# A transformer kernel on one core: expert rows gathered from two tables instead of one

## The reference, cut to what matters

```python
q = (xb @ wq).reshape(t, PEER_HEADS, 2, PEER_DQ // 2)
s = jnp.einsum('thpd,hpkd->thpk', q, subkeys).astype(jnp.float32)
s_top, i_top = lax.top_k(s, K)
cand = (s_top[:, :, 0, :, None] + s_top[:, :, 1, None, :]).reshape(t, PEER_HEADS, K * K)
c_top, c_idx = lax.top_k(cand, K)
...
e = i1 * N_KEYS + i2
g = jax.nn.softmax(c_top, axis=-1)
ue = jnp.take(u, e, axis=0)
ve = jnp.take(v, e, axis=0)
act = jax.nn.gelu(jnp.einsum('thkd,td->thk', ue, xb).astype(jnp.float32), approximate=False)
return jnp.einsum('thk,thkd->td', (g * act).astype(xb.dtype), ve)
```

## Time and profile before

| | |
|---|---|
| median of two runs | 1958.32 us |
| the two runs | 1958.12 and 1958.52 us |
| span of the profiled execution | 1954.8 us |
| time around the span (median less span) | 3.5 us |
| busy: PE, DVE, ACT, POOL | 1688.8, 1292.9, 926.7, 826.3 us |
| bytes moved | 637.60 MB, mean 326 GB/s |
| issues of expert rows | 512 |
| granted TensorE clock | 0.987 of full, the level of 2.4 GHz, in all stages |

### The profile page before, as it was taken

How to read it: one execution, slowest core, us unless ns; L and a number is a source line. 1 busy time by engine, 2 the same in 40 slices (tenths; PEclk the granted TensorE clock), 3 DMA queues, 4 the chain that set the end, 5 groups by cost and what they waited for, 6 DMA issues and landing times.

```text
span 1954.8 us, 22618 instructions
## 1 busy us (share of the span) xinstructions
PE 1688.8 (86%) x7638; PEld 1040.0 (53%) x7638; DVE 1292.9 (66%) x2806; ACT 926.7 (47%) x2424; POOL 826.3 (42%) x756
## 2 busy tenths in 40 slices
PE   7998998877787788799899999989989778787777
PEld 7996444422332222399899999974444223232222
DVE  4568777666776665558745784488767666666644
ACT  5456554444544444466525344465454444444443
POOL 3335334433333333277615474653434333343331
PEclk9999999999999999999999999999999999999999
DMA  7548999999999999654303334789999999999996
GB/s 250 184 159 325 414 421 421 421 421 421 421 421 421 422 421 422 274 167 155 108 22 99 119 95 139 264 302 414 422 420 421 422 421 422 422 420 422 422 421 290
DMA packets 102052, 637.60 MB, mean 326 GB/s; under 512 B 11264, under 2 KB 12544, under 8 KB 36144
## 3 DMA queue, kind: packets, MB, share of 16 engines
q0 software_dynamic: 75216, 543.73, 67.1%
q1 hardware_dynamic: 26720, 92.43, 14.5%
HBM read 635.07 MB, written 1.05 MB: 325 GB/s over the span
## 4 chain that ended last, share of the span: by engine, by line
PE 42%; DMA 36%; DVE 12%; ACT 8%; issue 2%; POOL 0%; SPq 0%; ACTq 0%; DVEq 0%
DMA arena<-in_uv,arena 34%; PE pb L657 17%; PE pb L397 6%; PE pb L399 5%; PE pb L398 5%; DVE arena L1817 4%; ACT arena L1112 3%; PE pb L476 1%; PE pb L872 1%; DVE parts L1385 1%; DMA spare<-in_uv,arena 1%; PE pb L794 1%; PE pb L785 1%; ACT parts L958 1%; ACT arena L1107 1%
## 5 line engine op out<-in xcount | busy, mean ns | idle before, releaser
L657 PE MATMUL pb<-arena 128*128 128x512 f32 x1904 | 931.3, 620 | 209.7 <-ACT arena L1112 208.6
L1817 DVE SCALAR_TENSOR_TENSOR arena<-arena,pb 128x1024 f32<-128x1024 f32 x476 | 580.3, 1219 | 372.2 <-DMA arena<-in_uv,arena 372.0
L2325 POOL DMA_INDIRECT arena<-in_uv,arena x476 | 450.4, 946 | 726.4 <-PE pb L657 694.9
L657 PEld LDWEIGHTS pb<-arena 128*128 128x128 f32 x1904 | 332.5, 191 | 766.6 <-ACT arena L1112 510.0
L2299 POOL TENSOR_TENSOR parts<-ring,parts 128x512 fp32r<-128x512 f32 x222 | 327.9, 1500 | 312.5 <-ACT parts L958 311.5
L1104 ACT ACTIVATE arena<-arena 128x1 f32<-128x1 f32 x512 | 103.1, 201 | 579.5 <-DVE arena L1817 532.9
L958 ACT ACTIVATE parts<-ring 128x512 fp32r<-128x512 f32 x300 | 180.4, 627 | 174.0 <-PE pb L399 149.1
L397 PE MATMUL pb<-xl,parts 128*128 128x256 f32 x704 | 220.6, 313 | 11.3 <-POOL parts L2299 4.4
L1112 ACT ACTIVATE arena<-cst,arena 128x128 f32<-128x128 f32 x512 | 205.5, 401 | 48.3 <-ACT arena L1107 1.9
L399 PE MATMUL pb<-xh,parts 128*128 128x256 f32 x704 | 201.4, 286 | 0.0
L398 PE MATMUL pb<-xh,parts 128*128 128x256 f32 x704 | 201.3, 286 | 0.0
(11 more groups left out here) (329 smaller groups left out, 1677.5 us busy)
## 6 DMA issues: line engine op xcount, KB each, us to landing
ring<-in_w_in SPq DMA_DIRECT2D x108, 512.0 KB, 3.6
ring<-in_wq SPq DMA_DIRECT2D x18, 512.0 KB, 4.4
ring<-in_w_out SPq DMA_DIRECT2D x16, 512.0 KB, 3.8
arena<-in_uv,arena POOLq DMA_INDIRECT x476, 20.1
arena<-in_wq SPq DMA_DIRECT2D x10, 512.0 KB, 5.7
ring<-in_wa SPq DMA_DIRECT2D x8, 512.0 KB, 3.7
ring<-in_wb SPq DMA_DIRECT2D x8, 512.0 KB, 3.6
spare<-in_wq SPq DMA_DIRECT2D x4, 512.0 KB, 4.9
```

The lines of the kernel that those rows point to most:

```text
L657: ins = pe.matmul(ys[hf][:, :], diags[:, k % 4, :], lands[land_of[k]][:, D + hf * 512:D + (hf + 1) * 512], start=False, stop=k % (8 * K) = ...
L1817: ve.scalar_tensor_tensor(z, z, 1.0, xg[t], ALU.mult, ALU.mult, accum_out=hidden[:, k:k + 1]).then_inc(*up("v_dot", ("dot", e, k)))
L2325: gp.indirect_dma_start(lands[land_of[k]], None, rows_uv, bass.IndirectOffsetOnAxis(ap=eidx[:, k:k + 1], axis=0)).then_inc(*up(f"dma_rows{ ...
```

## The change

The table `uv` is given up for two tables, `u` and `v`, of 4 KB rows. Each slot takes two indirect DMAs with the same column of indices: first the `u` row into the first half of the place, with the semaphore and key `rows`, then the `v` row into the second half, with a new semaphore for each place and the key `values`. The dot product still waits for `rows`, which now stands for the first half alone. The matmuls wait for `values` as well as the diagonal. SP's wait before the second block's weights is now for the last `values`. The same bytes are moved.

```diff
--- before.py
+++ after.py
@@ -653,6 +653,7 @@
                         lend(("xg", e, 1), (0, 1))
                         ys = sums_begun(1)
                     pq.wait_ge(*on(("diag", e, k)))
+                    pq.wait_ge(*on(("values", e, k)))
                     for hf in range(2):
                         ins = pe.matmul(ys[hf][:, :], diags[:, k % 4, :], lands[land_of[k]][:, D + hf * 512:D + (hf + 1) * 512],
                                         start=False, stop=k % (8 * K) == 8 * K - 1)
@@ -2306,7 +2307,7 @@
             gp.dma_start(wab[:, :], d["wab"]).then_inc(*up("dma_wab", "ld_wab", 16))
             ahead(18 * 4 - PARTS + 4)
 
-            def experts(e, wq, out_features, sk, normed_rows, final_rows, rows_uv):
+            def experts(e, wq, out_features, sk, normed_rows, final_rows, rows_u, rows_v):
                 gq.wait_ge(*on(("full", (out_features, 3))))
                 gp.dma_start(keys.rearrange("p (b c) n -> p b (c n)", b=2), sk.rearrange("b p n -> p b n")).then_inc(
                     *up("dma_keys", ("keys", e), 16))
@@ -2322,11 +2323,14 @@
                         if land_used[k] is None and land_of[k] >= 7 and (plan[h][0], (n + 1) // 2) == (wq, land_of[k] - 6):
                             for p in pieces_of[h]:
                                 gq.wait_ge(*on(("lo", p)))
-                    gp.indirect_dma_start(lands[land_of[k]], None, rows_uv,
+                    gp.indirect_dma_start(lands[land_of[k]][:, 0:D], None, rows_u,
                                           bass.IndirectOffsetOnAxis(ap=eidx[:, k:k + 1], axis=0)).then_inc(
                         *up(f"dma_rows{land_of[k]}", ("rows", e, k), 16))
-
-            experts(1, "wq", "w_out", d["sk"], d["ffn1"], d["fin1"], d["uv"])
+                    gp.indirect_dma_start(lands[land_of[k]][:, D:2 * D], None, rows_v,
+                                          bass.IndirectOffsetOnAxis(ap=eidx[:, k:k + 1], axis=0)).then_inc(
+                        *up(f"dma_values{land_of[k]}", ("values", e, k), 16))
+
+            experts(1, "wq", "w_out", d["sk"], d["ffn1"], d["fin1"], d["u"], d["v"])
 
 
 
@@ -2355,7 +2359,7 @@
             for _ in range(len(fillers) - EARLY - 1):
                 item()
             ahead(8 * 4 - PARTS + 4)
-            experts(2, "wq2", "w_out2", d["sk2"], d["ffn2"], d["fin2"], d["uv2"])
+            experts(2, "wq2", "w_out2", d["sk2"], d["ffn2"], d["fin2"], d["u2"], d["v2"])
 
 
 
@@ -2386,7 +2390,7 @@
                     for p in pieces_of[before]:
                         sq.wait_ge(*on(("lo", p)))
                 if (name, i) == ("w_in2", 0):
-                    sq.wait_ge(*on(("rows", 1, NT * 8 * K - 1)))
+                    sq.wait_ge(*on(("values", 1, NT * 8 * K - 1)))
                 sp.dma_start(ring_of(k), d[name][i]).then_inc(*up(f"w_slot{ring_no[k] % SLOTS}", None, 16))
             for t in range(NT):
                 for hf in range(2):
...
```

More of the change, by code:

```diff
@@ L2443, in weight @@
         return np.ascontiguousarray(w.transpose(3, 0, 2, 1, 4)).reshape(2 * n, P, 1024)
-    def side_by_side(u, v):
-        return np.concatenate([u.reshape(P * P, D), v.reshape(P * P, D)], axis=1)
     def keys(s):
@@ L2472 @@
         "w_in": weight(a["w_in"][0], 14), "w_out": weight(np.roll(a["w_out"][0], 512, axis=0), 4), "wq": weight(a["peer_wq"][0], 8),
-        "sk": keys(a["peer_subkeys"][0].reshape(16, P, P)), "uv": side_by_side(a["peer_u"][0], a["peer_v"][0]),
+        "sk": keys(a["peer_subkeys"][0].reshape(16, P, P)), "u": a["peer_u"][0].reshape(P * P, D), "v": a["peer_v"][0].reshape(P * P, D),
         "ffn1": np.broadcast_to(a["norm_ffn_g"], (P, D)), "ffn2": np.broadcast_to(a["norm2_2"], (P, D)),
@@ L2476 @@
         "w_out2": weight(a["w_out_2"][0], 4), "wq2": weight(a["w_pq_2"][0], 8), "sk2": keys(sk2),
-        "uv2": side_by_side(a["expert_u_2"][0], a["expert_v_2"][0]),
+        "u2": a["expert_u_2"][0].reshape(P * P, D), "v2": a["expert_v_2"][0].reshape(P * P, D),
     }
```

## The result

| | before | after |
|---|---|---|
| median of the runs | 1958.32 us | 2174.70 us (2173.96 and 2175.45) |
| ratio, 95% interval | | 1.1095 (1.1077 to 1.1113) |
| span of the profiled execution | 1954.8 us | 2173.6 us |
| granted TensorE clock, mean | 0.987 | 0.905 |

The changed kernel is 216 us slower. I had forecast 45, and 2174.7 lies far outside my range of 1973 to 2032: the direction was right, the size was not. The 171 us that are missing are over four times the largest term of my sum (38.4).

The account below looks back on a forecast made before the run. The prediction took the 16 full DMA engines in the two expert stages as the bound, 2.492 us a slot. 38.4 + 9 - 2.6 = 45 us, with span 1954.8 and 3.5 around it, made 2003 us, range 1973 to 2032.

Parts of the forecast that it names:

- Packets: Expert stages' gathers: two 4 KB packets cost 1.03 times one of 8 KB, 0.075 us more a slot, 38.4 us.
- the 408 GB/s: Sign in the plateaus: DMA share stays at 1.00 and the rate falls from 421 to about 408 GB/s.
- GpSimd's issues: Each slot takes two indirect issues of 1.247 us, so GpSimd needs 2.49 us a slot instead of 1.25.
- Ten stops of GpSimd at fixed counts: GpSimd's five stops a stage, 2.3 us each, go by instruction count and become ten, 23 us a stage.
- my own sign of a forecast that is wrong altogether: GpSimd's stops don't double, or the issue of a half costs less than 0.94 us.
- The coupling: DMA and GpSimd paths without reserve lose a quarter of long slot waits: 4.4 us a stage, 9 in all, at most 17.5 a stage.
- Rival 3: GpSimd becomes the bound, stops and slot waits exposed: stage 686 instead of 653 us, +66 in all, 2024; chance 0.17.
- share below 0.97 with GpSimd busy without gaps: Sign that GpSimd has become the bound: DMA share drops below 0.97 while GpSimd is busy without gaps.
- The split's gain: At each stage's end the last dot product starts before the second half lands: 1.3 us gained a stage, 2.6 in all.
- rule of at least 1 MiB a DMA: Skill page's rule, about 2 us fixed for each DMA: 3.2 us for each half megabyte if run one after another.

Follow-up runs that it names:

- e8: Kernel before, with only the odd slots fetched as two gathers of 4 KB rows from separate tables, on one semaphore: 1980.5 us (ratio 1.0116).
- e5: Kernel before, with a second gather of 128 rows of 64 bytes behind the odd slots' gathers only: 1983.9 us (ratio 1.0133).
- e10: Changed kernel, with a 0.84 us subtraction on GpSimd in front of every second slot's gathers, a break after four gathers: 2137.9 us.
- e4: Kernel before, with a second gather of 128 rows of 64 bytes, read by nobody, behind every slot's gather: 2155.0 us.
- e12: Kernel before, with only each stage's last slot split into two gathers, its dot product behind the first half: 1955.6 against 1959.2 us.
- e1: Changed kernel, with both gathers of a slot on one semaphore, the dot product waiting for both and no extra TensorE wait: 2167.4 us.
- e3: Changed kernel with seven places instead of ten, so at most 14 gathers in flight instead of 20: 2171.7 us.
- e11: Changed kernel with five places instead of ten, so at most ten gathers in flight: 2172.9 us.
- e7: Kernel before, with a 0.84 us subtraction on GpSimd behind every slot's gather and no further DMA: 1970.9 us (ratio 1.0065).
- e6: Kernel before, with a second gather of 128 rows of 64 bytes in three slots of four: 2015.9 us (ratio 1.0297).
- e9: Changed kernel, with a 0.84 us subtraction on GpSimd in front of every fourth slot's gathers, a break after eight gathers: 2167.3 us.

## Why the prediction was wrong, step by step

- **Packets (38.4 us): right in size.** e8 has 0.072 us for a split slot, 37 us for all 512, though e5 finds the same price without smaller packets; the fed slices of the kernel after reach the 408 GB/s and a little more.
- **GpSimd's issues (2.49 us a slot, 485 us more busy time): right.** The gaps of 0.30 us are there.
- **Ten stops of GpSimd at fixed counts, 23 us a stage: wrong.** In e10, where hardly a signal is late and GpSimd never waits long, its waits named issue are 0.3 us at the longest. I had read five waits of the kernel before as something that goes with the count of instructions. What they are is open. In the first stage of the kernel after, too, GpSimd has four waits named issue above 0.31 us (2.88, 2.04, 1.74 and 0.71) and not ten. The stops don't double, which was my own sign of a forecast that is wrong altogether.
- **The coupling (9 us, at most 17.5 a stage): here the forecast failed.** I bounded what two queues without a reserve could do to each other by the waits of the kernel before, as if a wait could only be lost. That bound rested on signals that take as long as before. With 2.564 us of DMA and 2.49 of GpSimd, on-time signals leave the pace at 2.564; measured are 2.907. The 0.343 between them are 176 us over 512 slots, which I had at 9, and e4 has some 160 us beyond its own DMA time without a single 4 KB packet. Rival 3 had the place right, a GpSimd without a reserve, and a price of a third of the loss (66 us for GpSimd's path with all its stops and waits exposed); its mechanism, stops and long waits of the kernel before, was not the one. My sign for it, "share below 0.97 with GpSimd busy without gaps", is half true: the share is 0.94, but GpSimd's gaps are what shows.
- **The split's gain (1.3 us a stage): too large.** e12 has 0.74 in its trace, since TensorE then has two slots' matmuls to do at once; e1, which waits for both halves, is not slower than the kernel after.
- The Trainium skill's rule of at least 1 MiB a DMA (page "DMA: Bandwidth & Descriptors", section "Measured (HBM→SBUF, 128 partitions, SWDGE, issued from GpSimd)"), which I had weighed against the plateau, doesn't explain the loss. In e8 half-megabyte gathers run at 415 GB/s, since the queue is fed.

The sum: 37 us for the split gathers' DMA time + 176 us = 213 us, beside 216. The 176 are what the pace in the middle of a stage has beyond on-time signals, a difference and not a sum of waits, so this is no second proof.

**Shown**: the second gather costs nearly the whole (e4); not by its bytes (e4), its wait or semaphore (e1) or the depth (e3, e11), nor by GpSimd's load as such (e10, and e7 with a reserve), nor in proportion (e5, e6); with a break of 1 us after four gathers the late signals all but end (e10), after eight they don't (e9). **Not shown**: whether it is the unbroken issuing or the rate of gathers, about 0.7 a us, that makes signals late, and by what path it holds up the signals of engines that have nothing to do with GpSimd. The stop at 710 ended while GpSimd stood still, the wait at 759 while it issued, so the traces don't say that it must stop first. Nor is it excluded that recording takes a part: every execution here has a recorded span and clock, and where signals are late over half of the updates that DMAs make are missing from the trace; but in e10, with signals on time, 8708 of 19,456 are missing too. A second transfer on another queue was not tried.

## What to carry to other kernels

An issuing queue whose load goes to 100% is not priced by its busy time: between three quarters and all of GpSimd's time in indirect gathers the loss went from 25 to 197 us, and it fell on engines that never touch that queue. Before splitting a gather, count the issues for each period of the loop; here a quarter of GpSimd's time free (0.59 gathers a us) was enough and an eighth (0.68) was not; and if a wait named "remote" appears on one core, look for an instruction that waits for its own engine's signal alone, since it tells a late signal from late work. Split only the transfer whose first part ends a stage.

## What the hardware showed that I had not expected

- A signal from VectorE to itself arrived 4.5 us late (709.43 to 713.93), and those from TensorE at least 7.3 us (706.55 to 713.91), all at once, behind a run of indirect gathers that GpSimd issued 0.30 us apart; 147 such waits and 636.7 us in a run, none in the kernel before.
- Adding 213 us of arithmetic to the queue that issues the gathers took 37 us off the time.
- Every kernel with many late signals ran at 0.68 to 0.70 gathers a us, whatever its places, semaphores or row sizes.
- A gather into 64 partitions ran at 231 GB/s, with packets of 8 KB at 0.58 us; into 128 partitions the same packet took 0.315.
- Two gathers of 4 KB rows take 1.03 times the DMA time of one of 8 KB rows (2.564 beside 2.492 us a slot), and a gather of 64-byte rows beside the whole one takes as much (0.074 us).
